# Token halves across the seam between two layers, with GpSimd adding residuals and squares

## The chip, the cores and the metric

The kernel runs on one core of one Trainium2 chip. Its time is the device time of one execution in microseconds (us). A core has five engines with queues of their own that meet only through semaphores: TensorE (PE in the rows; PEld is its weight load), VectorE (DVE), ScalarE (ACT), GpSimd (POOL) and SyncE (SP). Matmuls write to PSUM, the others read from it (POOL doesn't in this kernel). Before the change the median of three runs was 1852.86 us.

## The reference

Two transformer blocks over 512 tokens of width 2048, in float32. Around the change it computes the end of the first block and the start of the second:

```python
def _rms_norm(x, g):
    xf = x.astype(jnp.float32)
    y = xf * lax.rsqrt(jnp.mean(xf * xf, axis=-1, keepdims=True) + NORM_EPS)
    return (y * g.astype(jnp.float32)).astype(x.dtype)

def _hybrid_layer(...):          # first block
    ...
    o = jnp.concatenate([o_mla, o_fox], axis=-1) @ w_out
    return x + _rms_norm(o, g_post)

def second_block(x, ...):
    ...
        h = _rmsnorm(x, norm_g[l])
        proj = h @ w_in[l]
```

The first block's output projection `o @ w_out` needs all of its 2048 columns before the norm of a token is known; then the residual x is added, and the result is both the residual of the second block and, normed, the input of its projection.

## The kernel before, in words

Activations lie transposed: the feature on the partitions, 16 tiles (`KT`) of 128 features, each 512 tokens wide (`S`). A float32 product is made of three matmuls (`three`, L421 to L423): high part times high part, low part of the activation (`xl`) times high part of the weight, and high part (`xh`) times low part of the weight (`wl`). Weights come in units of 128 x 1024 through four slots of `raw`, `wh` and `wl`: SP loads `raw`, ACT rounds it to `wh` (L979, `act_hi`), DVE forms `wl` = raw - wh (L1433, `lo`), PE uses both and counts `w_used`, and then the slot may be refilled. Each engine works through a list written out by hand; the order in the code is the order on the engine, and semaphores count.

The first output projection makes 16 strips of 128 output features, each from 16 x 3 matmuls of 512 columns into one of two PSUM banks. DVE copies a strip out (L1902), ACT squares it (L1241), DVE adds the squares into `acc` (L1896). After strip 15 PE sums `acc` and the last squares over the partitions for each of four groups of 128 tokens (`pe_token_sums`, L552 and L556). DVE and ACT make the inverse root (`token_rms`, L1539 to L1547, with the square root at L1021) and put it on the diagonal of `gate` (L1550); PE spreads it over the partitions (`pe_spread`, L564) and runs six warm-up matmuls that nothing reads (L715).

Then every tile j goes through this chain: DVE scales it by g_post and the spread factor (L1924, `scale_tile`; the factor lies in PSUM); the residual is added, for tiles 0 and 1 by DVE from `xr1` (L1930), for tiles 2 to 15 by an accumulating DMA from DRAM that POOL's queue issues (L389); ACT makes `xh` (L1258) and the tile's squares (L1261); DVE makes `xl` (L1599, `x_rest`) and adds the squares (L1605, `square_in`). POOL also issues four stores of the new residual (L383). PE takes the tiles in order (`pe_four`): each is used at once for four outputs in four PSUM banks, 12 matmuls a tile. Two tiles use one weight unit, `U_CMPIN` + 0 to 7. Before unit 7 stands the sum over the squares (`pe_sum`, L546), which needs those of all 16 tiles; its result scales the projections that follow. At the very end of the kernel the same norm is already worked in two token halves, with strips of 256 columns (L960, L948, L952, L2248), and POOL scales some of the output tiles (L416).

Of the kernel before, what the change touches and what calls it, by code (L numbers as in the profile page):

```python
# [20 lines left out]
F32 = mybir.dt.float32  # L21
# [70 lines left out]
WARM_FIRST, WARM_MID = 5, 6  # L92
# [37 lines left out]
def _build(nc, d, ctx):  # L130
# [43 lines left out]
    sq = [place("sq0", [P, S], offset=at["prob"] + 2048), place("sq1", [P, S], offset=at["prob"] + 4096)]  # L174
# [43 lines left out]
    xr1 = place("xr1", [P, 2, S], offset=at["y"])  # L218

# [5 lines left out]
    kv0 = at["next"]  # L225

# [81 lines left out]
    scaled, part_done = sem("scaled"), sem("part_done")  # L308
    low_out, low_in = sem("low_out"), sem("low_in")
# [3 lines left out]
    four_done, raw_first, first_hi, first_lo = sem("four_done"), sem("raw_first"), sem("first_hi"), sem("first_lo")  # L313
    block = ctx.enter_context(nc.Block())
# [50 lines left out]
    def _(g):  # L365
# [9 lines left out]
        g.dma_start(xr1[:, :, :], d["xt"][:, 0:2, :]).then_inc(xr1_in, 16)  # L375
        g.dma_start(cos2[:, :], d["cos_a"]).then_inc(tab2_in, 16)
        g.dma_start(sin2[:, :], d["sin_a"]).then_inc(tab2_in, 16)

        def x_is_added(j):
            g.wait_ge(x_added[j % 4], 16 * (j // 4 + (j % 4 >= 2)))  # L380
# [167 lines left out]
    def pe_token_sums(pe, i, squared):  # L548

        pe.wait_ge(acc_ready, i + 1)  # L550
        for t in range(NQ):
            pe.matmul(px[:, t:t + 1], acc[:, P * t:P * t + P], ones[:, 0:1], start=t == 0, stop=False,  # L552
                      skip_group_check=True)
# [6 lines left out]
    def pe_spread(pe, k_, banks):  # L560

        for out in banks:
            pe.wait_ge(diag_done, NQ * (k_ + 1))
            pe.matmul(out[:, :], ones[:, :], gate[:, :], start=True, stop=True).then_inc(spread, 1)  # L564

    @block.tensor
    def _(pe):
# [141 lines left out]
        with pe.Fori(1, KT // 2 - 1) as i:  # L709
# [172 lines left out]
        def b_pair(p, u, n_, steps):  # L882
# [38 lines left out]
        for steps, strips in ((range(12, 15), (0,)), (range(12, 15), (1,)), (range(15, KT), (0, 1))):  # L921
            pe_together(pe, U_OUT2, N_OUT2, steps, 4 * KT - 6, strips=strips)
# [21 lines left out]
        def half_sums(hf):  # L944

            pe.wait_ge(acc_ready, 6 + hf)
            for t in (2 * hf, 2 * hf + 1):
                pe.matmul(px[:, t:t + 1], acc[:, P * t:P * t + P], ones[:, 0:1], start=t == 2 * hf, stop=False,  # L948
                          skip_group_check=True)
            pe.wait_ge(ev_act, N_OUT2 + KT - 4 + 2 * hf)  # L950
            for t in (2 * hf, 2 * hf + 1):
                ins = pe.matmul(px[:, t:t + 1], e_t[:, P * t:P * t + P], ones[:, 0:1], start=False,  # L952
                                stop=t == 2 * hf + 1, skip_group_check=True)
            ins.then_inc(sum_done, 1)
# [69 lines left out]
    def _(a):  # L1024
# [221 lines left out]
        with a.Fori(0, KT // 2 - 1) as i:  # L1246
            two_strips(At(U_OUT1 + 4, i, 4), lambda j: out_square(
                N_OUT1 + 2 + j + i * 2, o[:, bass.ds(2 * i + 2 + j, 1), :].rearrange("p a n -> p (a n)")))
        act_hi(a, At(U_CMPIN + 2))
        act_hi(a, At(U_CMPIN + 3))  # L1250
        act_root(a, 3)

        for j in range(KT):
            if j < 2:
                a.wait_ge(xn_done, j + 1)
            else:
                a.wait_ge(x_added[j % 4], 16 * (j // 4 + (j % 4 >= 2)))
# [162 lines left out]
        for hf in range(2):  # L1420
# [3 lines left out]
            act_root(a, 5 + hf, 2 * hf, 2 * hf + 2)  # L1424
            a.wait_ge(spread, 2 + 2 * hf)
# [128 lines left out]
    def _(v_):  # L1554
# [343 lines left out]
        def out1(first, i, last=False, banks=(pj[N_OUT1 % 2], pj[1 - N_OUT1 % 2])):  # L1898
            def evac(j, used):
# [16 lines left out]
        two_strips(At(U_CMPIN - 4), out1(14, 0, True))  # L1916
        token_rms(v_, 3)
        v_.memset(acc[:, :], 0.0)
        lo(v_, At(U_CMPIN + 2))
        lo(v_, At(U_CMPIN + 3))  # L1920
        v_.wait_ge(spread, 1)

        def scale_tile(j):
            ins = v_.scalar_tensor_tensor(o[:, j, :], o[:, j, :], c("g_post", j), po[:, :], ALU.mult, ALU.mult)  # L1924
            if j >= 2:
                ins.then_inc(scaled, 1)

        def residual(j):
            v_.drain()
            v_.tensor_tensor(o[:, j, :], o[:, j, :], xr1[:, j, :], ALU.add).then_inc(xn_done, 1)  # L1930

        scale_tile(0)
        v_.wait_ge(xr1_in, 16)
        residual(0)
        scale_tile(2)
        scale_tile(1)
        x_rest(0, o[:, 0, :], c("g_2", 0), 3 * KT - 6)
        residual(1)
        scale_tile(3)
        for j in range(KT):  # L1940
            if j + 4 < KT:
                scale_tile(j + 4)
            if j:
                x_rest(j, o[:, j, :], c("g_2", j), 3 * KT - 6)
            if j:
                square_in(j - 1, KT)
            if j in (5, 7, 9, 11):
                lo(v_, At(U_CMPIN + (j + 3) // 2))
        square_in(KT - 1, KT)
# [456 lines left out]
```

## Time and profile before

| what | value |
|---|---|
| median of three runs | 1852.86 us (1852.66 to 1852.92) |
| the profiled execution | 1853.12 us, span 1851.4 us |
| PE, DVE, ACT, POOL busy | 98%, 57%, 36%, 2% of the span |
| last matmul of the first projection starts | 955.20 us |
| sum matmul before unit 7 starts | 1007.88 us |

The span runs from the first to the last instruction of the profiled execution; the time is a little longer. Times in the rows are microseconds from the span's start. A busy PE is a matmul in flight: records of neighbouring matmuls overlap, so the distance from start to start tells the rate. An idle time in brackets is what the engine waited before the row, and for whom.

### The profile page before, as it was taken

To read this page: it belongs to the slowest core of one execution; us is meant where nothing else is said; L and a number is where in the kernel's file an instruction comes from. 1 tells how busy PE (TensorE), PEld (TensorE's weight loads), DVE (VectorE), ACT (ScalarE), POOL (GpSimd) and SP (SyncE) were. 2 spreads that over 40 slices of the span, in tenths; PEclk is the share of its full clock that TensorE was granted. 3 is DMA by queue.
4 is the path that set the end of the run, shared out by engine and by line. 5 is a ranking of instruction groups with operands and counts; after the bars stand their busy time and mean duration, and the time that the engine had idled before them with its cause. 6 is when DMAs were issued, how large, how long until landed. Compare 5 with 4: busy or idle time off the path is not lost.

```text
span 1851.4 us, 25537 instructions
## 1 busy us (share of the span) xinstructions
PE 1823.4 (98%) x9060; PEld 1514.8 (82%) x9060; DVE 1047.4 (57%) x1768; ACT 665.6 (36%) x1279; POOL 36.3 (2%) x58
## 2 busy tenths in 40 slices
PE   9999999999999999999999999999999999999997
PEld 7788888888888887878868887888888888888887
DVE  7643434444433787853348954766767566665334
ACT  6532332322223544432226342433433333443222
POOL 0000000000000000000002000000000000000001
PEclk9999999999999999999999999999999999999998
DMA  6322222222232333232237363211112222124333
GB/s 237 106 86 91 79 79 91 86 84 82 89 102 80 126 114 113 91 112 93 91 101 218 102 227 124 70 57 57 68 57 69 92 68 79 66 70 136 115 115 102
DMA packets 56021, 186.16 MB, mean 101 GB/s; under 512 B 6688, under 2 KB 11168, under 8 KB 55456
## 3 DMA queue, kind: packets, MB, share of 16 engines
q1 hardware_dynamic: 51328, 170.78, 27.6%
q0 software_dynamic: 4640, 14.68, 3.0%
q8 instruction: 33, 0.54, 0.1%
q14 instruction: 20, 0.16, 0.0%
HBM read 177.05 MB, written 8.39 MB: 100 GB/s over the span
## 4 chain that ended last, share of the span: by engine, by line
PE 90%; DVE 5%; DVEq 2%; ACT 1%; issue 1%; POOL 0%; POOLq 0%; ACTq 0%
PE strip L421 23%; PE strip L423 22%; PE strip L422 22%; PE scores L421 4%; PE scores L422 3%; PE scores L423 3%; PE outputs L423 2%; PE outputs L422 2%; PE outputs L421 1%; PE scores L476 1%; PE scores L869 1%; PE scores L828 1%; PE scores L897 1%; DVE wl L1433 1%; DVEq L1438 0%
## 5 line engine op out<-in xcount | busy, mean ns | idle before, releaser
L421 PE MATMUL strip<-xh,wh 128*128 128x512 f32 (+1 forms) x1976 | 779.7, 395 | 5.7 <-DVE xl L1825 3.2
L423 PE MATMUL strip<-xh,wl 128*128 128x512 f32 (+1 forms) x1976 | 768.0, 389 | 0.0
L422 PE MATMUL strip<-xl,wh 128*128 128x512 f32 (+1 forms) x1976 | 767.2, 388 | 0.0
L421 PEld LDWEIGHTS strip<-xh,wh 128*128 128x128 f32 x1976 | 371.9, 188 | 82.4 <-DVE xl L1825 4.8
L423 PEld LDWEIGHTS strip<-xh,wl 128*128 128x128 f32 x1976 | 371.6, 188 | 77.3
L422 PEld LDWEIGHTS strip<-xl,wh 128*128 128x128 f32 x1976 | 372.3, 188 | 72.7 <-issue 0.7
L1433 DVE TENSOR_TENSOR wl<-raw,wh 128x1024 fp32r<-128x1024 f32 (+3 forms) x306 | 354.7, 1177 | 119.1 <-ACT wh L979 118.2
L979 ACT ACTIVATE wh<-raw 128x1024 fp32r<-128x1024 f32 (+3 forms) x308 | 306.9, 1023 | 109.7 <-PE strip L423 107.1
L1001 ACT ACTIVATE prob<-scores,nms 128x128 f32<-128x128 f32 (+3 forms) x128 | 65.9, 532 | 129.7 <-DVE nms L1481 129.7
L1241 ACT ACTIVATE e_t<-o 128x512 f32 (+1 forms) x30 | 19.0, 632 | 222.0 <-DVE o L1902 118.1
L421 PE MATMUL scores<-xh,wh 128*128 128x512 f32 (+1 forms) x240 | 91.6, 382 | 0.0
L423 PE MATMUL scores<-xh,wl 128*128 128x512 f32 (+1 forms) x240 | 90.1, 375 | 0.0
L422 PE MATMUL scores<-xl,wh 128*128 128x512 f32 (+1 forms) x240 | 90.0, 375 | 0.0
L1441 DVE TENSOR_TENSOR y<-strip,rb 128x512 f32<-128x512 f32 x45 | 31.1, 692 | 75.7 <-PE strip L423 73.1
L1479 DVE TENSOR_REDUCE nm<-scores 128x1 f32<-128x128 f32 (+1 forms) x96 | 41.2, 485 | 55.1 <-PE scores L457 54.3
L984 ACT ACTIVATE q_h<-y 128x512 fp32r<-128x512 f32 x24 | 15.2, 632 | 145.8 <-DVE y L1454 107.2
L994 ACT ACTIVATE e_t<-y 128x512 f32<-128x512 f32 x32 | 20.5, 641 | 127.4 <-DVE y L1441 127.4
L1505 DVE TENSOR_TENSOR ptl<-scores,pth 128x512 fp32r<-128x512 f32 (+3 forms) x128 | 53.8, 483 | 9.7 <-ACT pth L1009 9.6
L421 PEld LDWEIGHTS scores<-xh,wh 128*128 128x128 f32 x240 | 45.2, 188 | 9.0 <-issue 0.5
L422 PEld LDWEIGHTS scores<-xl,wh 128*128 128x128 f32 x240 | 45.2, 188 | 8.7 <-issue 0.7
L423 PEld LDWEIGHTS scores<-xh,wl 128*128 128x128 f32 x240 | 45.2, 188 | 8.1
L1902 DVE COPY o<-strip 128x512 f32 (+1 forms) x14 | 9.7, 692 | 74.0 <-PE strip L423 73.9
(426 smaller groups left out, 1875.6 us busy)
## 6 DMA issues: line engine op xcount, KB each, us to landing
raw<-in_w SPq DMA_DIRECT2D x308, 512.0 KB, 3.2
xn<-o POOLq DMA_DIRECT2D x4, 1024.0 KB, 7.8
xr<-xn POOLq DMA_DIRECT2D x16, 256.0 KB, 3.0
o<-in_xt SPq DMA_DIRECT2D x7, 512.0 KB, 7.9
o<-in_xt POOLq DMA_DIRECT2D x14, 256.0 KB, 6.3
out<-o SPq DMA_DIRECT2D x14, 256.0 KB, 2.7
raw<-in_w SPq DMA_DIRECT2D x2, 256.0 KB, 4.6
o<-in_xt SPq DMA_DIRECT2D x2, 256.0 KB, 5.1
```

The costliest lines, as they stand in the source:

```text
L421: pe.matmul(out, ah, bh, start=first, stop=False, skip_group_check=shared)
L422: pe.matmul(out, ah, bl, start=False, stop=False, skip_group_check=shared)
L423: return pe.matmul(out, al, bh, start=False, stop=last, skip_group_check=shared)
L476: ins = pe.transpose(sb[t][:, P * (w - t):P * (w - t) + P], prob[:, ROW[w] + P * t:ROW[w] + P * t + P], ident[:, :])
L979: a.activation(wh[s][:, :cols], raw[s][:, :cols], ACT.Copy).then_inc(w_hi, 1)
L994: a.activation(e_t[:, :], src, ACT.Tanh, scale=0.5).then_inc(ev_act, 1)
L1001: a.activation(prob[:, ROW[t]:ROW[t] + w], sb[t][:, pre[t]:pre[t] + w], ACT.Exp, bias=nms[:, t:t + 1], scale=scale, accum_out=lsum[:, t:t ...
L1241: a.activation(e_t[:, :], src, ACT.Square).then_inc(ev_act, 1)
L1433: v_.tensor_tensor(wl[s][:, :cols], raw[s][:, :cols], wh[s][:, :cols].bitcast(F32), ALU.subtract)\
L1441: v_.tensor_tensor(dst, src[:, :], times[:, :], ALU.mult).then_inc(y_done, 1)
L1479: v_.tensor_reduce(nm[:, t:t + 1], sb[t][:, 0:P * (t + 1)], AX.X, ALU.max, negate=True)
L1505: v_.tensor_tensor(ptl[:, cols], sb[t][:, 0:w], pth[:, cols].bitcast(F32), ALU.subtract)\
```

## The change

- The last two strips (14 and 15) are made in token halves of 256 columns: both for tokens 0 to 255 first, then both for tokens 256 to 511. The token sums of the first half stand inside strip 14's second half, and its spread ahead of strip 15's second half.
- The first six tiles (`HT`) of the second layer's input are scaled, added, split and multiplied in halves too: all six for the first half of the tokens, then all six for the second. The second half's token sums come after tile 1's first half, its spread after tile 3's. The warm-up matmuls are gone.
- The residuals of the six tiles come from `xr1`, now six tiles wide, and POOL adds them (12 additions of 256 columns). Tiles 6 to 15 still get theirs by an accumulating DMA.
- The sum of squares goes from DVE to POOL, into its own `acc_mid`: 12 additions of 256 columns and ten of 512. The sum matmul waits for POOL's last one. The squares have four buffers instead of two.

```diff
-        for j in range(2, KT):
-            if j >= 6:
-                x_is_added(j - 4)
-            g.wait_ge(scaled, j - 1)
-            g.dma_start(o[:, j, :], d["xt"][:, j, :], accum_op=ALU.add).then_inc(x_added[j % 4], 16)
-            if j == 7:
-                g.wait_ge(xn_done, 2)
-            if j in (7, 11, 15):
-                xn_store(j - 7)
+        def residual(hf, j):
+            g.wait_ge(scaled, HT * hf + j + 1)
+            part = o[:, j, TOKENS[hf]]
+            g.tensor_tensor(part, part, xr1[:, j, TOKENS[hf]], ALU.add).then_inc(xn_done, 1)
+        def x_added_in(j):
+            if j - 4 >= HT:
+                x_is_added(j - 4)
+            g.wait_ge(scaled, HT + j + 1)
+            g.dma_start(o[:, j, :], d["xt"][:, j, :], accum_op=ALU.add).then_inc(x_added[j % 4], 16)
+        def square_half(hf, j):
+            g.drain()
+            g.wait_ge(sq_done, KT + HT * hf + j + 1)
+            g.tensor_tensor(acc_mid[:, TOKENS[hf]], acc_mid[:, TOKENS[hf]], sq_part(hf, j), ALU.add).then_inc(sq_used, 1)
+        def square(j):
+            g.drain()
+            g.wait_ge(sq_done, KT + HT + j + 1)
+            g.tensor_tensor(acc_mid[:, :], acc_mid[:, :], sq[j % 4][:, :], ALU.add).then_inc(sq_used, 1)
...
+        for j in range(HT, KT):
+            if j + 4 < KT:
+                x_added_in(j + 4)
+            if j == 8:
+                xn_store(4)
+            if j == 12:
+                xn_store(8)
+            square(j)
...
-        pe_token_sums(pe, 3, N_OUT1 + KT)
-        pe_spread(pe, 0, (po,))
-        for i in range(WARM_MID):
-            pe.matmul(px[:, :], ones[:, :], gate[:, :], start=True, stop=True)
-        pe_four(pe, U_CMPIN, 3 * KT - 6, sb, summed=(4, 7))
+        out1_half(0, 0, range(KT))
+        out1_half(0, 1, range(KT))
+        out1_half(1, 0, range(5))
+        pe_half_sums(pe, 0, 4, (half_sq, 2))
+        out1_half(1, 0, range(5, KT))
+        pe.wait_ge(diag_done, 2)
+        pe.matmul(po[:, 0:256], ones[:, :], gate[:, 0:256], start=True, stop=True).then_inc(spread, 1)
+        out1_half(1, 1, range(KT))
+        def aside(j):
+            if j == 1:
+                pe_half_sums(pe, 1, 5, (ev_act, N_OUT1 + KT))
+            if j == 3:
+                pe.wait_ge(diag_done, NQ)
+                pe.matmul(px[:, :], ones[:, :], gate[:, :], start=True, stop=True).then_inc(spread, 1)
+        pe_mid(pe, U_CMPIN, sb, aside)
...
+        for hf in range(2):
+            for j in range(HT):
+                pe.wait_ge(x_lo, X_MID + HT * hf + j + 1)
+                if hf == 0 and j % 2 == 0:
+                    pe.wait_ge(w_lo, u0 + j // 2 + 1)
+                for s in range(4):
+                    ins = tile(j, s, TOKENS[hf], hf == 0 and j == 0, False)
+                if hf == 1 and j % 2 == 1:
+                    ins.then_inc(w_used, 1)
+                if hf == 0:
+                    aside(j)
+        for u in range(HT // 2, 8):
+            if u == 7:
+                pe.wait_ge(sq_used, KT + HT + KT)
+                pe.matmul(px[:, :], ones[:, :], acc_mid[:, :], start=True, stop=True).then_inc(sum_done, 1)
...
+            scale_half(1, j)
+        rest_half(1, 0)
+        scale_half(1, 3)
+        rest_half(1, 1)
+        scale_half(1, 4)
+        rest_half(1, 2)
+        scale_half(1, 5)
+        scale_tile(6)
+        rest_half(1, 3)
+        scale_tile(7)
+        rest_half(1, 4)
+        rest_half(1, 5)
+        lo(v_, At(U_CMPIN + 4))
+        scale_tile(8)
+        scale_tile(9)
+        for j in range(HT, KT):
+            x_rest(j, o[:, j, :], c("g_2", j), X_MID + HT)
             if j + 4 < KT:
                 scale_tile(j + 4)
-            if j:
-                square_in(j - 1, KT)
```

ACT's list follows: half squares for the strips, then `xh_half` and `sq_half` for the six tiles, with the second half's square root behind `xh_half(0, 5)`.

POOL's queue at this place, before. `in_xt` is the first layer's input in DRAM, `xn` the new residual in DRAM:

```order
L389 DMA o<-in_xt 128x512 x6
L383 DMA xn<-o 128x2048
L389 DMA o<-in_xt 128x512 x4
L383 DMA xn<-o 128x2048
L389 DMA o<-in_xt 128x512 x4
L383 DMA xn<-o 128x2048 x2
```

The same place after, from the second half's third residual on (`xr_135` is `xr1`, `sq_87` and `sq_88` are two of the four buffers of squares):

```order
L392 TENSOR_TENSOR o<-o,xr_135 128x256
L401 DMA o<-in_xt 128x512
L392 TENSOR_TENSOR o<-o,xr_135 128x256
L401 DMA o<-in_xt 128x512
L392 TENSOR_TENSOR o<-o,xr_135 128x256
L406 TENSOR_TENSOR acc_mid<-acc_mid,sq_87 128x256
L392 TENSOR_TENSOR o<-o,xr_135 128x256
L401 DMA o<-in_xt 128x512
L406 TENSOR_TENSOR acc_mid<-acc_mid,sq_88 128x256
L401 DMA o<-in_xt 128x512
L406 TENSOR_TENSOR acc_mid<-acc_mid,sq_88 128x256
```

The DMA issues now stand in one queue with additions: residuals ahead of each issue, and sums of squares between them.

DVE's list before, once the factor is spread:

```order
L1924 SCALAR_TENSOR_TENSOR o<-o,cvec,outputs 128x512
L1930 TENSOR_TENSOR o<-o,xr_128 128x512
L1924 SCALAR_TENSOR_TENSOR o<-o,cvec,outputs 128x512 x2
L1599 SCALAR_TENSOR_TENSOR xl<-o,cvec,xh 128x512
L1930 TENSOR_TENSOR o<-o,xr_128 128x512
L1924 SCALAR_TENSOR_TENSOR o<-o,cvec,outputs 128x512 x3
L1599 SCALAR_TENSOR_TENSOR xl<-o,cvec,xh 128x512
L1605 TENSOR_TENSOR acc<-acc,sq_85 128x512
```

DVE's list after, once the second half's factor is spread (L2076 scales a half tile, L2085 a whole one, L2081 makes half of `xl`, L1584 is `lo`):

```order
L2076 SCALAR_TENSOR_TENSOR o<-o,cvec,odds 128x256 x3
L2081 SCALAR_TENSOR_TENSOR xl<-o,cvec,xh 128x256
L2076 SCALAR_TENSOR_TENSOR o<-o,cvec,odds 128x256
L2081 SCALAR_TENSOR_TENSOR xl<-o,cvec,xh 128x256
L2076 SCALAR_TENSOR_TENSOR o<-o,cvec,odds 128x256
L2081 SCALAR_TENSOR_TENSOR xl<-o,cvec,xh 128x256
L2076 SCALAR_TENSOR_TENSOR o<-o,cvec,odds 128x256
L2085 SCALAR_TENSOR_TENSOR o<-o,cvec,odds 128x512
L2081 SCALAR_TENSOR_TENSOR xl<-o,cvec,xh 128x256
L2085 SCALAR_TENSOR_TENSOR o<-o,cvec,odds 128x512
L2081 SCALAR_TENSOR_TENSOR xl<-o,cvec,xh 128x256 x2
L1584 TENSOR_TENSOR wl_59<-raw_51,wh_55 128x1024
```

The residual and the sum of squares are gone from DVE; tile 6's scaling stands behind three halves of `xl`, and tile 8's behind all six and a weight unit.

## Rows read from the trace of the kernel before

**Rows 1.** The page's first part: busy time, share and instructions of each engine.
```profile
PE 1823.4 (98%) x9060; PEld 1514.8 (82%) x9060; DVE 1047.4 (57%) x1768; ACT 665.6 (36%) x1279; POOL 36.3 (2%) x58
```
**Rows 2.** Windows: length, busy of PE, PEld, DVE, ACT, POOL, clock, DMA share, GB/s.
```profile
940.00:955.40 15.40, 15.40 (x69) 12.78 (x68) 3.75 (x4) 2.53 (x3) 0.00 (x0) 1.00 0.36 115
955.40:969.40 14.00, 10.42 (x32) 5.45 (x30) 10.63 (x22) 5.10 (x8) 1.46 (x2) 0.76 0.34 90
```
**Rows 3.** Window of DVE alone: length, DVE busy, clock, DMA share, GB/s.
```profile
969.30:1003.90 34.60, 32.81 (x46) 1.00 1.01 259
```
**Rows 4.** Timeline of PE at the gap and the sum: start, duration, instruction.
```profile
939.79 0.39 PE L421 MATMUL strip<-xh,wh 128*128 128x512 f32 x1
...
955.20 0.39 PE L423 MATMUL strip<-xh,wl 128*128 128x512 f32 x1
...
969.36 0.80 PE L421 MATMUL scores<-xh,wh 128*128 128x512 f32 x1
969.99 0.39 PE L422 MATMUL scores<-xl,wh 128*128 128x512 f32 x1
...
1007.88 1.02 PE L546 MATMUL odds<-acc,ones 128*128 128x512 f32 x2
...
1008.97 0.40 PE L422 MATMUL scores<-xl,wh 128*128 128x512 f32 x1
```
**Rows 5.** Timeline of PE near the end: half strips, half sums between, half spread.
```profile
1824.27 0.28 PE L421 MATMUL scores<-xh,wh 128*128 128x256 f32 x1
...
1827.03 0.28 PE L423 MATMUL scores<-xh,wl 128*128 128x256 f32 x1
...
1827.96 0.36 PE L421 MATMUL scores<-xh,wh 128*128 128x256 f32 x1
...
1830.91 0.60 PE L960 MATMUL outputs<-gate,ones 128*128 128x256 f32 x2
...
1831.47 0.28 PE L422 MATMUL scores<-xl,wh 128*128 128x256 f32 x1
```
**Rows 6.** Timeline of DVE and POOL near the end: operations of 256 columns, gate.
```profile
1821.42 0.43 DVE L2257 TENSOR_TENSOR acc<-acc,e_t 128x256 f32<-128x256 f32 x1 [2.22 <-ACT e_t L1423]
...
1828.57 0.17 DVE L1541 RECIPROCAL rinv<-nms 128x2 f32<-128x2 f32 x1 [0.27 <-ACT nms L1021]
...
1829.52 0.48 DVE L1550 TENSOR_SCALAR gate<-ident,rinv 128x128 f32<-128x128 f32 x2
...
1832.08 3.71 POOL L416 TENSOR_TENSOR o<-o,rb 128x256 f32<-128x256 f32 x5 [17.06 <-ACT rb L1426]
1832.27 0.83 DVE L2257 TENSOR_TENSOR acc<-acc,e_t 128x256 f32<-128x256 f32 x1 [0.73 <-ACT e_t L1423]
1833.23 4.40 DVE L2242 SCALAR_TENSOR_TENSOR o<-o,cvec,outputs 128x256 f32<-128x256 f32 x11
...
1843.60 3.45 POOL L416 TENSOR_TENSOR o<-o,rb 128x256 f32<-128x256 f32 x5 [7.82 <-ACT rb L1426]
```
**Rows 7.** Timeline in the second layer's input: one tile's xh, one weight remainder.
```profile
970.50 0.72 ACT L1258 ACTIVATE xh<-o,cvec 128x512 fp32r<-128x512 f32 x1 [1.34 <-DMA o<-in_xt]
...
980.00 1.22 DVE L1433 TENSOR_TENSOR wl<-raw,wh 128x1024 fp32r<-128x1024 f32 x1
```
**Rows 8.** Tile o on POOL: minimum, median, maximum of the operation (ns), of landing (us).
```profile
L416 POOL TENSOR_TENSOR o<-o,rb x10: 722/730/914, 1832.1 to 1846.3; 128x256 f32<-128x256 f32 x10
...
DMA to landing us min/median/max: 4.2/6.5/9.4
```
**Rows 9.** POOL's memsets (group and timeline) and two DMA issues in a row.
```profile
L366 POOL MEMSET nrt<- 128x512 f32 x1 | 0.5, 524 | 0.3 <-POOLq L2397 0.3
...
800.21 0.95 POOL L374 MEMSET blk<- 128x1024 f32 x1 [752.76 <-DVE o L1512]
...
974.61 0.87 POOL L389 DMA_DIRECT2D o<-in_xt  x1 [1.24 <-DVE o L1924]
975.15 0.89 POOL L383 DMA_DIRECT2D xn<-o  x1
```

More of the change, by code:

```diff
@@ L225, in _build @@
     kv0 = at["next"]
+    xr1 = place("xr1", [P, HT, S], offset=kv0)
     def group_kv(g, where):
@@ new lines, in _ @@
+        for j in range(HT):
+            residual(0, j)
+            if j >= 3:
+                square_half(0, j - 3)
+        residual(1, 0)
+        square_half(0, 3)
+        residual(1, 1)
+        square_half(0, 4)
+        residual(1, 2)
+        x_added_in(6)
+        residual(1, 3)
+        x_added_in(7)
+        residual(1, 4)
+        square_half(0, 5)
+        residual(1, 5)
+        x_added_in(8)
+        square_half(1, 0)
+        x_added_in(9)
+        for j in range(1, HT):
+            square_half(1, j)
@@ L546, in pe_sum, with pe_half_sums @@
         pe.matmul(px[:, :], ones[:, :], squares[:, :], start=True, stop=True).then_inc(sum_done, 1)
[L548 to L552, printed above, removed]
+    def pe_half_sums(pe, hf, added, squared):
+        pe.wait_ge(acc_ready, added)
+        for t in (2 * hf, 2 * hf + 1):
+            pe.matmul(px[:, t:t + 1], acc[:, P * t:P * t + P], ones[:, 0:1], start=t == 2 * hf, stop=False,
@@ L553, in pe_token_sums, with pe_half_strip @@
                       skip_group_check=True)
-        pe.wait_ge(ev_act, squared)
-        for t in range(NQ):
-            ins = pe.matmul(px[:, t:t + 1], e_t[:, P * t:P * t + P], ones[:, 0:1], start=False, stop=t == NQ - 1,
+        pe.wait_ge(*squared)
+        for t in (2 * hf, 2 * hf + 1):
+            ins = pe.matmul(px[:, t:t + 1], e_t[:, P * t:P * t + P], ones[:, 0:1], start=False, stop=t == 2 * hf + 1,
                             skip_group_check=True)
         ins.then_inc(sum_done, 1)
[L560 to L564, printed above, removed]
+    def pe_half_strip(pe, u0, out, hf, steps):
+        for k_ in steps:
+            u = u0 + k_ // 8
+            if k_ % 8 == 0:
+                pe.wait_ge(w_lo, u + 1)
+            cols = slice(P * (k_ % 8), P * (k_ % 8) + P)
+            ins = three(pe, out[:, 0:256], wh[u % SLOTS][:, cols], wl[u % SLOTS][:, cols], xh[:, k_, TOKENS[hf]],
+                        xl[:, k_, TOKENS[hf]], k_ == 0, k_ == KT - 1)
+            if hf == 1 and k_ % 8 == 7:
+                ins.then_inc(w_used, 1)
+        if hf == 0 and k_ == KT - 1:
+            ins.then_inc(part_done, 1)
@@ L944, in half_sums @@
         def half_sums(hf):
[L946 to L954, printed above, removed]
+            pe_half_sums(pe, hf, 6 + hf, (ev_act, N_OUT2 + KT - 4 + 2 * hf))
         def half_spread(hf, banks):
@@ L1896, in add_square, with out1 @@
             v_.tensor_tensor(acc[:, :], acc[:, :], e_t[:, :], ALU.add).then_inc(r_done, 1)
-        def out1(first, i, last=False, banks=(pj[N_OUT1 % 2], pj[1 - N_OUT1 % 2])):
+        def out1(first, i, banks=(pj[N_OUT1 % 2], pj[1 - N_OUT1 % 2])):
             def evac(j, used):
@@ L1915, in _ @@
             two_strips(At(U_OUT1 + 4, i, 4), out1(2, i))
-        two_strips(At(U_CMPIN - 4), out1(14, 0, True))
-        token_rms(v_, 3)
-        v_.memset(acc[:, :], 0.0)
+        for j in range(2):
+            lo(v_, At(U_CMPIN - 2 + j))
+        out1_half(0, 0)
+        half_add(0)
+        out1_half(0, 1)
+        token_rms(v_, 3, 0, 2)
+        out1_half(1, 0)
+        v_.wait_ge(spread, 1)
+        scale_half(0, 0)
+        scale_half(0, 1)
+        half_add(1)
+        v_.drain().then_inc(r_done, 1)
@@ L1923, in scale_tile @@
[L1923 to L1937, printed above, removed]
@@ L1938, in _ @@
-        residual(1)
-        scale_tile(3)
-        for j in range(KT):
+        v_.wait_ge(spread, 2)
+        for j in range(3):
+            scale_half(1, j)
[13 more added lines that the diff above has]
+        scale_tile(9)
```

199 lines of the change are left out of this document (152 added, 47 removed).

## The prediction

> **What bounds the kernel now.** I read the page first. TensorE (PE) is busy 98% of the span and VectorE (DVE) 57%, ScalarE 36%, GpSimd (POOL) 2% [rows 1]. So a change pays only where PE does no useful matmuls, or costs where it makes PE wait. The table by stage shows the place [rows 2]: before 955.4 us PE is full at a granted clock of 1.00; from 955.4 to 969.4 it is busy 10.42 of 14.00 us at 0.76; then it is full again. Then the timeline of PE [rows 4]: the last strip matmul starts at 955.20; token sums, the wait for the root, the spread and six warm-up matmuls fill the gap; the first matmul of the second layer is recorded at 969.36, the one behind it at 969.99. At one matmul per 0.2266 us (below) the last strip matmul ends its turn at 955.43 and the first new one really ran at 969.76. The useful work stops for 14.33 us. From there to the sum matmul at 1007.88 PE waits for nothing, while DVE is nearly full (32.81 of 34.60 us) [rows 3] and POOL only issues DMAs.
>
> **PE's own ledger.** 512-column matmuls come every (955.20 - 939.79)/68 = 0.2266 us [rows 4]; 256-column ones every (1827.03 - 1824.27)/23 = 0.120 us [rows 5]. Two strips (96) and six tiles of four outputs (72) are split: 168 x (2 x 0.120 - 0.2266) = +2.25 us. Two half token sums now lie between matmuls: 1827.96 - (1827.03 + 0.12) = 0.81 each, 1.62 [rows 5]. The 256-column spread costs (1831.47 - 1830.91) - 0.12 = 0.44 [rows 5]. The 512-column one costs what the sum matmul does, 1008.97 - 0.23 - 1007.88 = 0.86 [rows 4]. Together 5.17 us, against 14.33 removed (the warm-ups lie in these). If PE never waited, the sum would start 9.16 us earlier, at 998.7, and the kernel would take 1843.7. All that follows asks whether the others can feed it.
>
> **The first halves.** The strips begin at 955.43 - 96 x 0.2266 = 933.68. The first half's spread comes after 144 half matmuls and the sums: 951.8 to 952.2. Scaling takes 0.40 a half tile (4.40/11) [rows 6], so POOL gets its first residual at 952.9. POOL's 256-column op comes every 3.45/5 = 0.69 us [rows 6]. Until residual 5 it has eight ops (six residuals, two adds): 5.5 us.
>
> Now the port. The group of five POOL ops during which a DVE add with two SBUF inputs ran took 3.71 us, the other 3.45; that DVE add took 0.83 us, and 0.43 when POOL was still; the eleven DVE ops whose factor lay in PSUM kept 0.40 [rows 6]. So two-input DVE ops and POOL's take turns, and POOL lost 0.26, the add's 256 elements at about 1 ns. I scale it by elements: 0.27 for 256, 0.53 for 512, 1.07 for 1024. The Trainium skill (SBUF — State Buffer, Who interferes with whom) states this as an exclusive lock, in which the later of the two blocks fully; the trace agrees, and the rule speaks against this change, since it puts tensor work on POOL beside a DVE that makes weight and activation remainders from two SBUF inputs. Without turns the sum would be the first rival's.
>
> POOL loses three weight remainders (3.2) and six small ones (1.6), and waits 0.7 for scaling: residual 5 ends at 952.9 + 5.5 + 3.2 + 1.6 + 0.7 = 963.9. Behind it on ScalarE's queue stand xh (0.72 for a whole tile [rows 7]; a half is put at six tenths of it, 0.43) and then the square root of the second half's sums, put at 0.2 for two columns; DVE's small ops and two gates take (1829.52 + 0.48) - 1828.57 = 1.43 [rows 6]: gate ready at 966.1. PE, which ends its last half strip at 933.68 + 23.04 + 0.81 + 0.44 = 957.97, wants it after four half tiles and the sums, at 964.5. It waits 1.6 us. The spread ends at 967.0, DVE does one rest and one weight remainder before scaling, and POOL starts the second halves at 968.2.
>
> **POOL's ledger from 968.2 to the sum,** which now waits for POOL's last add:
> - six residuals x 0.69 = 4.1
> - nine half adds x 0.73 (each waits for the one before to end, 0.722 in the trace [rows 8]) = 6.6
> - ten whole-tile adds: no 512-column POOL op with two inputs is in the trace. Between 0.72 (size costs nothing) and 1.44 (twice the record). The two memsets, 0.524 for 512 columns and 0.95 for 1024 [rows 9], leave a fixed 0.1; (0.69 - 0.1) x 2 + 0.1 = 1.28, I take 1.30: 13.0
> - ten accumulating DMAs and three stores: between 0.54 (975.15 - 974.61, two starts in a row) and 0.87 (a record's length) [rows 9]; nearer to neither, I take 0.70: 9.1
> - three times POOL stands still because the tile whose DMA is next is scaled only behind rests that wait for POOL's own residual: xh 0.43, rest 0.43, scale 0.40, tile scale 0.74, with handoffs 2.3; the next without the half scale 1.9; the third with a weight remainder of 1.22 [rows 7], 3.0: 7.2
> - DVE's two-input ops in this stretch: 6 x 0.27 + 4 x 1.07 + 10 x 0.53 = 11.2. Some fall while POOL issues or idles, and some wait for POOL instead. Between 0 and 11.2; I take two fifths, 4.5.
> Sum 44.5: the sum matmul starts at 1012.7 instead of 1007.88, +4.8 us. Unit 7's 24 matmuls behind it and all that follows hang on it as before.
>
> The Trainium skill (GPSIMD Engine Reference, Elementwise — side-by-side cycle accounting) gives about 2.6 cycles an element and 4497 ns for 2048; an estimate from it for 512 is near 1.2 us. No row here shows one, and with it the sum would be about 1 us less.
>
> DVE loses 16 adds of 0.69 and two residuals; this is worth nothing, since it now waits for POOL. Four accumulating DMAs of 256 KB fewer relieve a stage whose DMA share is 1.01 [rows 3]; their landing, 4.2 to 9.4 us [rows 8], stays under the four-tile lead, so I count nothing. The longer xr1 load is issued behind the memset of 800.21 us [rows 9], 150 us ahead: nothing; its cover would have to shrink by all of that.
>
> The profiled execution took 1853.12 for a span of 1851.4; the median of the three runs is 1852.86. The difference applies to all alike: 1852.86 + 4.8 = 1857.7.
>
> **Rivals.**
> 1. *The turns at the port cost little.* For it: most POOL time in the trace is undisturbed. Against: the 0.83. Then 4.5 goes, and of the first halves' 4.8 the 1.6 that PE waited: 1857.7 - 6.1 = 1851.6.
> 2. *PE stays the bound* (the other side). Mechanism: DMA issues run under the adds (0.54 and overlapped), a whole add is near 0.9, and POOL's still times are covered. POOL must save 1012.7 - 998.7 = 14.0: issues 7, adds 4, port 3. It decides once POOL's last add ends before 998.7. Time 1844; half of that saving still gives about 1850.7.
> 3. *POOL at its upper bounds:* issues at 0.87 (+2.2), adds 1.44 (+1.4), port seven tenths (+3.3): 1864.6; with half of it 1861.
> 4. *The clock.* Over the gap of before, where PE stood and then ran warm-ups, the granted clock was 0.76, between its two levels [rows 2]. PE would now wait in bits of 2 us with work between, so I expect 1.00; if it lost as much as in the gap, 0.24 of 14 us, 3.4 go unless POOL is late anyway: 1861 at most.
>
> **Chances.** This kernel can be told from no change by about 0.2%, 3.7 us: faster is below 1849.2, slower above 1856.6. Forecast 0.55 (own range 1854 to 1861; 0.12 of it below 1856.6), rival 1 0.19 (same but 0.02), rival 2 0.16, rivals 3 and 4 0.10. Slower 0.43 + 0.10 = 0.53; faster 0.18; same 0.29. The range leaves out the upper part of rival 3 and the lower of rival 2: 1847.5 to 1862.
>
> **What would show it.** Right: POOL nearly full from 968 to 1012; the sum matmul idle before it, with POOL's whole-tile add as releaser; half tiles of the second half waiting on xl; DVE's two-input ops longer than 0.75 and 1.22 beside POOL's; whole POOL adds near 1.3. Wrong: no idle time of PE after 957 (rival 2), POOL ops at 0.69 with DVE ops at their old lengths (rival 1), a granted clock under 1.00 between 966 and 990 (rival 4), or PE waiting for the DMAs of tiles 6 to 15, which I have at nothing.

## The result, and the profile after

The changed kernel took 1898.94 us (median of four runs, 1898.39 to 1899.32), the kernel before on the same chip 1852.89 (1852.66 to 1853.4): ratio 1.0248, 95% interval 1.023 to 1.0266. The forecast was 1857.7. The sign was right, and the loss is 46 us where 4.8 were forecast. The profiled execution took 1898.84 us with a span of 1897.1.

The profile of the changed kernel is called after. Its page, busy time, share and instructions of each engine, beside [rows 1]:

```profile
PE 1827.5 (96%) x9218; PEld 1524.0 (80%) x9218; DVE 1044.5 (55%) x1769; ACT 669.1 (35%) x1294; POOL 66.5 (4%) x89
```

PE's busy time is nearly what it was; 46 us were added in which it stands. The table of waits of PE from 930 to 1100 us (line, releaser, total us, times, longest):

```profile
PE scores L474 <- DVE xl L1750: 19.4, 5, 6.3
PE odds L649 <- POOL acc_mid L411: 15.8, 1, 15.8
PE scores L474 <- DVE xl L2081: 6.6, 3, 2.4
PE odds L833 <- DVE gate L1701: 1.4, 1, 1.4
```

The same table for POOL:

```profile
POOL o L392 <- DVE o L2076: 154.5, 4, 149.9
POOL acc_mid L411 <- issue: 31.0, 10, 6.9
POOL acc_mid L406 <- issue: 12.1, 12, 4.0
POOL o L401 <- DVE o L2085: 7.6, 3, 3.2
```

Here lies the answer. The three waits for `L2085` (the scaling of a whole tile) are the 7.6 us that the forecast had as 7.2. But 43.1 us stand ahead of the 22 square adds with "issue" as their releaser, which means that no semaphore in the profile ended them. The instruction in front of each add is `g.drain()`. The timeline of POOL shows what it waited for (start, duration, instruction, idle before it):

```profile
968.36 0.74 POOL L392 TENSOR_TENSOR o<-o,xr 128x256 f32<-128x256 f32 x1 [3.24 <-DVE o L2076]
969.25 0.74 POOL L406 TENSOR_TENSOR acc_mid<-acc_mid,sq 128x256 f32<-128x256 f32 x1 [0.16 <-issue]
...
987.50 0.87 POOL L401 DMA_DIRECT2D o<-in_xt  x1 [3.16 <-DVE o L2085]
992.41 0.73 POOL L406 TENSOR_TENSOR acc_mid<-acc_mid,sq 128x256 f32<-128x256 f32 x1 [4.05 <-issue]
993.10 0.86 POOL L401 DMA_DIRECT2D o<-in_xt  x1
997.49 0.71 POOL L406 TENSOR_TENSOR acc_mid<-acc_mid,sq 128x256 f32<-128x256 f32 x1 [3.53 <-issue]
998.37 0.72 POOL L406 TENSOR_TENSOR acc_mid<-acc_mid,sq 128x256 f32<-128x256 f32 x1 [0.17 <-issue]
...
1001.95 0.60 POOL L414 DMA_DIRECT2D xn<-o  x1
1002.54 0.89 POOL L401 DMA_DIRECT2D o<-in_xt  x1
1010.33 1.26 POOL L411 TENSOR_TENSOR acc_mid<-acc_mid,sq 128x512 f32<-128x512 f32 x1 [6.90 <-issue]
...
1031.19 0.86 POOL L401 DMA_DIRECT2D o<-in_xt  x1
1035.48 1.27 POOL L411 TENSOR_TENSOR acc_mid<-acc_mid,sq 128x512 f32<-128x512 f32 x1 [3.44 <-issue]
1036.71 0.85 POOL L401 DMA_DIRECT2D o<-in_xt  x1
```

Behind additions only, the idle time ahead of an add is 0.16 us. Right behind an accumulating DMA it is 3.4 to 4.1 us, behind a 1 MB store and such a DMA 6.9, behind such a DMA and a store 5.65 (the add of 1024.25). A DMA lands when its data have arrived and its semaphore has counted them. ScalarE waits for just that before it makes `xh` of a tile, so its rows tell the time of the landing:

```profile
1035.33 0.72 ACT L1410 ACTIVATE xh<-o,cvec 128x512 fp32r<-128x512 f32 x1 [3.43 <-DMA o<-in_xt]
```

The tile issued at 1031.19 has landed by 1035.33, and POOL's add starts at 1035.48. The same holds for the other whole adds that have a tile's DMA right in front of them: each starts 0.15 to 0.19 us behind ScalarE's start on that tile. So the drain ends with the landing. A queue in which issue and landing overlapped has become a chain: issue, landing, add, next issue. Its period is 1036.71 - 1031.19 = 5.5 us a tile, 8.3 to 9.0 where a store lies in it; PE needs 12 x 0.2266 = 2.7 us a tile.

PE at the spread and at the sum, timeline (answers to [rows 4]):

```profile
966.41 1.13 PE L833 MATMUL odds<-gate,ones 128*128 128x512 f32 x2 [1.40 <-DVE gate L1701]
...
1052.24 2.08 PE L649 MATMUL odds<-acc_mid,ones 128*128 128x512 f32 x2 [15.78 <-POOL acc_mid L411]
```

And the windows of after in the columns of [rows 2]:

```profile
955.40:970.00 14.60, 13.20 (x106) 12.52 (x105) 13.20 (x25) 8.11 (x18) 9.06 (x10) 1.00 0.39 126
970.00:990.00 20.00, 11.87 (x82) 10.33 (x81) 9.90 (x17) 7.72 (x15) 8.07 (x10) 1.00 0.33 68
990.00:1010.00 20.00, 11.93 (x43) 8.99 (x42) 6.10 (x8) 3.95 (x6) 6.84 (x9) 0.83 0.58 143
1010.00:1052.00 42.00, 16.38 (x48) 11.76 (x48) 10.62 (x10) 11.29 (x15) 17.61 (x17) 0.68 0.42 106
```

The gap itself is filled: 13.20 of 14.60 us at a clock of 1.00, where it was 10.42 of 14.00 at 0.76. What was won there is lost from 970 on. No engine is full there: POOL, which the table of waits names, is busy 17.6 of 42 us. When neither PE nor its releaser is busy, the time goes into a wait that the busy times don't hold.

### The profile page after: what moved, and what is told of

Same layout as the page of the kernel before. It is cut to its first block, busy times and chain, and to the rows that moved or that the text cites. A ratio compares the mean times of both kernels' runs of the same rounds, so it can differ in the third digit from the quotient of the medians.

```text
span 1897.1 us, 25891 instructions
## 1 busy us (share of the span) xinstructions
PE 1827.5 (96%) x9218; PEld 1524.0 (80%) x9218; DVE 1044.5 (55%) x1769; ACT 669.1 (35%) x1294; POOL 66.5 (4%) x89
## 4 chain that ended last, share of the span: by engine, by line
PE 83%; DVE 6%; issue 4%; DVEq 2%; ACT 2%; POOL 1%; POOLq 1%; DMA 0%; SPq 0%; ACTq 0%
PE strip L474 22%; PE strip L476 22%; PE strip L475 22%; PE scores L474 2%; PE scores L475 2%; PE scores L476 2%; PE outputs L476 2%; PE outputs L475 2%; PE outputs L474 1%; PE scores L529 1%; DVE wl L1584 1%; PE scores L988 1%; PE scores L947 1%; PE scores L1016 1%; POOLq L404 1%
## 5 line engine op out<-in xcount | busy, mean ns | idle before, releaser
L474 PEld LDWEIGHTS strip<-xh,wh 128*128 128x128 f32 x2008 | 377.9, 188 | 81.5 <-DVE xl L1976 4.8
L476 PEld LDWEIGHTS strip<-xh,wl 128*128 128x128 f32 x2008 | 377.5, 188 | 76.3
L475 PEld LDWEIGHTS strip<-xl,wh 128*128 128x128 f32 x2008 | 378.1, 188 | 71.6 <-issue 0.7
L1584 DVE TENSOR_TENSOR wl<-raw,wh 128x1024 fp32r<-128x1024 f32 (+3 forms) x306 | 355.8, 1180 | 120.9 <-ACT wh L1090 120.0
L474 PE MATMUL scores<-xh,wh 128*128 128x512 f32 (+1 forms) x264 | 100.5, 381 | 26.6 <-DVE xl L1750 19.7
L475 PE MATMUL scores<-xl,wh 128*128 128x512 f32 (+1 forms) x264 | 96.8, 367 | 0.0
L476 PE MATMUL scores<-xh,wl 128*128 128x512 f32 (+1 forms) x264 | 96.6, 366 | 0.0
L474 PEld LDWEIGHTS scores<-xh,wh 128*128 128x128 f32 x264 | 51.6, 196 | 39.6 <-DVE xl L1750 23.3
L475 PEld LDWEIGHTS scores<-xl,wh 128*128 128x128 f32 x264 | 51.7, 196 | 8.2 <-issue 0.8
L476 PEld LDWEIGHTS scores<-xh,wl 128*128 128x128 f32 x264 | 51.4, 195 | 8.0
L1120 ACT ACTIVATE pth<-scores 128x512 fp32r<-128x512 f32 (+3 forms) x128 | 45.1, 437 | 12.3 <-PE scores L947 9.7
```

The source lines that it names most:

```text
L474: pe.matmul(out, ah, bh, start=first, stop=False, skip_group_check=shared)
L475: pe.matmul(out, ah, bl, start=False, stop=False, skip_group_check=shared)
L476: return pe.matmul(out, al, bh, start=False, stop=last, skip_group_check=shared)
L1120: a.activation(pth[:, COL[t]:COL[t] + w], sb[t][:, 0:w], ACT.Copy).then_inc(pt_hi, 1)
L1584: v_.tensor_tensor(wl[s][:, :cols], raw[s][:, :cols], wh[s][:, :cols].bitcast(F32), ALU.subtract)\
```

## The experiments

**1. Another wait in place of the drain.** Theory A: the drain waits for POOL's own DMAs. Theory B: POOL's work itself (adds, issues, the port) is dearer than forecast. All 22 drains become a wait on the semaphore that the add before has raised:

```diff
         def square_half(hf, j):
-            g.drain()
+            g.wait_ge(sq_used, KT + HT * hf + j)
...
         def square(j):
-            g.drain()
+            g.wait_ge(sq_used, KT + HT + j)
```

> The changed kernel with POOL's 22 drains ahead of its adds replaced by a wait on the semaphore that the add before it counts (sq_used); nothing else. Theory A (the drain holds POOL until its own accumulating DMAs have landed, 4.2 to 4.9 us each): the 41 us beyond my forecast go, POOL's ledger holds, about 1857.7 (1854 to 1862), and POOL's idle times of 3.4 to 7.8 us ahead of its adds shrink below 1 us save for the three waits for scaling. Theory B (POOL's adds are late for another reason: the landing of tiles' DMAs and ScalarE's waits for the square buffers): stays above 1890.

Measured 1864.89 us (1863.74 to 1865.43), ratio 1.0063 [1.0046, 1.0079]. 34.1 of the 46 us are gone with nothing else changed, and theory B's 1890 is far off; but the time stands 2.9 us above theory A's range, so something else was mis-sized too. POOL now issues while the adds run:

```profile
992.80 0.60 POOL L414 DMA_DIRECT2D xn<-o  x1
993.39 0.89 POOL L401 DMA_DIRECT2D o<-in_xt  x1
993.97 1.63 POOL L411 TENSOR_TENSOR acc_mid<-acc_mid,sq 128x512 f32<-128x512 f32 x1
995.21 1.23 POOL L401 DMA_DIRECT2D o<-in_xt  x1
```

The waits of PE from 930 to 1100 us:

```profile
PE scores L474 <- DVE xl L1750: 6.2, 2, 4.3
PE scores L474 <- DVE xl L2081: 3.8, 2, 2.4
PE odds L649 <- POOL acc_mid L411: 2.0, 1, 2.0
PE odds L833 <- DVE gate L1701: 1.3, 1, 1.3
```

**2. The drain alone, in the kernel before.** One drain behind each accumulating DMA, nothing else of the change:

```diff
             g.dma_start(o[:, j, :], d["xt"][:, j, :], accum_op=ALU.add).then_inc(x_added[j % 4], 16)
+            g.drain()
```

> The kernel before, with one drain on POOL behind each of the 14 accumulating DMA issues; no other change. Theory A: each issue follows the landing of the one before, one tile per about 4.4 + 0.5 = 4.9 us, the last lands near 966 + 14 x 4.9 = 1034.6 instead of about 1001; PE starts the sum near 1036 to 1038 instead of 1007.9: 1880 to 1884. Theory B: a drain costs 0.16 us as behind an add and is hidden: 1853.

Measured 1891.91 us (1889.67 to 1893.15), ratio 1.0212 [1.0195, 1.0229]: 39 us slower, 8 above the top of what was expected, with no additions on POOL in this stage. Its timeline:

```profile
981.99 0.86 POOL L389 DMA_DIRECT2D o<-in_xt  x1 [3.67 <-issue]
...
996.79 0.56 POOL L383 DMA_DIRECT2D xn<-o  x1 [4.12 <-issue]
997.34 0.90 POOL L389 DMA_DIRECT2D o<-in_xt  x1
1004.75 0.86 POOL L389 DMA_DIRECT2D o<-in_xt  x1 [6.51 <-issue]
```

Much the same 3.7 to 4.4 us ahead of the next issue, and 6.5 with a store in front. So the cost is the drain's, and needs neither an add nor a busy port. The expectation was too low because it left out the stores: with one in front of a DMA the step to the next issue is 7.4 us (1004.75 - 997.34) instead of 4.9, and that happens twice; the first issue was also 1.4 us later than assumed. The sum matmul starts at 1043.88.

**3. Only the half adds keep their drains.** Experiment 1's edit in `square` alone, so twelve of 22 stay:

```diff
         def square(j):
-            g.drain()
+            g.wait_ge(sq_used, KT + HT + j)
```

> The changed kernel with the drains ahead of the ten whole-tile adds replaced by the wait on the add before; the 12 drains ahead of half adds stay, three of which stand behind a DMA issue. Theory A: in the trace of the changed kernel those three waited 2.52, 4.05 and 3.53 us (10 together) and the whole-tile ones 31 us in all; so most of the loss goes and some 5 to 10 us stay against the kernel without any: 1863 to 1868. Theory B: no change from 1899.

Measured 1871.25 us (1870.47 to 1874.97), ratio 1.0105 [1.0088, 1.0122]. The ten drains of the whole-tile adds cost 27.7 us, the twelve others 6.4: 34.1 together. Of the twelve, three stand behind an issue (of tiles 7, 8 and 9); in after these three waited 2.52, 4.05 and 3.53 us. The time is 3.3 us above the expected range. The 6.4 us lie within the 5 to 10 expected; the kernel without any drain, to which they are added, came out slower than assumed.

**4. The stores out of the way.** Experiment 1 still stood 7.2 us above the forecast. Its longest wait of PE:

```profile
1003.98 0.50 PE L474 MATMUL scores<-xh,wh 128*128 128x512 f32 x1 [4.29 <-DVE xl L1750]
```

This is behind tile 10, whose DMA was issued at 993.39 right behind the 1 MB store of 992.80. On ScalarE, `xh` of that tile began when it had landed:

```profile
1002.42 0.72 ACT L1410 ACTIVATE xh<-o,cvec 128x512 fp32r<-128x512 f32 x1 [8.89 <-DMA o<-in_xt]
```

That is 9.0 us from issue to landing, against 4.2 us for the median of these DMAs in after. Experiment 4 takes experiment 1 and moves the four stores of `xn` behind the last accumulating DMA:

```diff
         g.wait_ge(xn_done, 2 * HT)
-        xn_store(0)
...
-            if j == 8:
-                xn_store(4)
-            if j == 12:
-                xn_store(8)
...
-        xn_store(12)
+        for k0 in range(0, KT, 4):
+            xn_store(k0)
```

> The kernel without POOL's drains (e1_sem_for_drain), with the four 1 MB stores of the new residual moved behind the last accumulating DMA instead of between them. Theory A (in e1 the store issued 0.6 us ahead of tile 10's accumulating DMA makes that land 9.0 us after its issue, and PE waits 4.3 us for tile 10): landing near 5 us, PE's wait goes: about 1861 (1864.9 less 4). Theory B (the landing is slow since the DMA engines are full of weights): 1865 as before.

Measured 1861.61 us (1860.88 to 1862.05), ratio 1.0044 [1.0027, 1.0061]: 3.3 us less, as expected. Tile 10's DMA, issued at 993.55, had landed when its `xh` began at 997.72, and PE's longest wait is 2.6 us, at a half tile. The weights are loaded as before and only the store has moved, so theory B falls. Whether the place in the queue or the store's mere traffic slowed the landing isn't told apart: from 993.5 to 1002.4 us the DMA share is 0.82, in experiment 1 it was 0.94.

**5. POOL without the sums.** Experiment 1 with all 22 adds in DVE's list (the stores as in the change). The line taken out is POOL's, the new ones are DVE's:

```diff
-            square(j)
...
+            if j < 9:
+                square_half(1, 2 * (j - 6))
+                square_half(1, 2 * (j - 6) + 1)
```

> e1_sem_for_drain with all 22 additions of squares moved from POOL to DVE's list (same tiles, same accumulator, stores where they are); POOL keeps 12 residuals, the DMAs and stores. Theory A (POOL's additions and their turns at the port cost PE time): the 2.0 us wait ahead of the sum and part of the waits for tiles go, 1858 to 1861. Theory B (the chain of scaling, residual, xh, xl and the landing alone holds PE): 1864 to 1866, PE's waits at the same tiles.

Measured 1859.87 us (1859.32 to 1861.01), ratio 1.0037 [1.0023, 1.0051]. 5.0 us less than experiment 1, within theory A's range. But the wait ahead of the sum did not go: PE now waits 2.8 us there for DVE's last add, so DVE is late in turn. What went is the long wait at tile 10, with the stores where they were: PE's longest wait at a whole tile is 1.4 us. POOL, free of adds, issues tile 10 at 986.91 instead of 993.39. So the adds and the store share that wait, and the gains of experiments 4 and 5 can't be added.

**6. DVE scales one or two places sooner,** on top of experiment 4, and POOL issues tiles 6 and 7 one residual later, so that no issue stands in front of a residual that DVE's next rest needs:

```diff
-        rest_half(1, 0)
         scale_half(1, 3)
-        rest_half(1, 1)
+        rest_half(1, 0)
         scale_half(1, 4)
-        rest_half(1, 2)
         scale_half(1, 5)
+        rest_half(1, 1)
         scale_tile(6)
```

> e4_stores_last with another order: DVE scales the half tiles 3 to 5 and the whole tiles 6 to 9 one or two places earlier, ahead of the rests that wait for POOL, and POOL does residual 3 ahead of tile 6's DMA issue. Theory A (my term of 7.2 us: POOL stands still for scalings that stand behind its own residuals): PE's waits at the fourth, fifth and seventh tile of the second half, 5.7 us in e1, mostly go: 5 us under e4, about 1856. Theory B (a wait that only moves): within 1.5 us of e4.

Measured 1856.55 us (1855.2 to 1858.18, ten runs), ratio 1.0016 [1.0006, 1.0026]: 5.1 us less than experiment 4. POOL stood still ahead of its DMA issues for 9.4 us in four places in experiment 4 and for 3.0 us in two here, and PE's waits for halves of `xl` fell from 5.0 to 2.1 us. The forecast had seen these waits, at 7.2 us. The edit moves items of both lists, so DVE's share and POOL's are not told apart.

**7. The ten whole-tile adds on DVE,** on top of experiment 6; POOL keeps residuals and half adds.

```diff
-            square(j)
...
+            for t in {9: (6,), 10: (7, 8), 11: (9,), 12: (10,), 13: (11,), 14: (12, 13), 15: (14,)}.get(j, ()):
+                square_tile(t)
+        square_tile(15)
```

> e6_scale_ahead with the ten whole-tile additions of squares moved from POOL to DVE; the 12 half additions stay on POOL. Theory A (what is left over the kernel before is POOL's queue: in e6 PE waits 1.9 us for POOL ahead of the sum, and 0.6 and 1.3 for tiles 10 and 11, whose xl and DMA issue stand behind POOL's whole adds): 1856.6 less 2 to 4, so 1853 to 1854.5. Theory B (DVE takes the same time with them): 1856 to 1858, the sum waiting for DVE.

Measured 1852.79 us (1849.46 to 1854.09) against 1854.13 for the kernel before in this comparison, ratio 0.9992 [0.9983, 1.0001]: equal. That is 3.8 us under experiment 6, where 2 to 4 were expected. PE's waits are down to 4.7 us in four places:

```profile
PE scores L469 <- DVE xl L2076: 2.1, 1, 2.1
PE odds L828 <- DVE gate L1696: 1.3, 1, 1.3
PE scores L469 <- DVE xl L1745: 0.7, 1, 0.7
PE odds L644 <- DVE acc_mid L2084: 0.6, 1, 0.6
```

**8. The second half's spread sooner,** on top of 7. The root stands one place earlier on ScalarE, POOL's first adds stand behind all six residuals, and one weight remainder behind the second halves. Theory A: the gate comes early enough and its wait goes. Theory B: it doesn't matter.

```diff
             residual(0, j)
-            if j >= 3:
-                square_half(0, j - 3)
+        for j in range(3):
+            square_half(0, j)
```

> e7_whole_adds_on_dve with the second half's norm sooner: its root on DVE and ScalarE ahead of the last two half tiles of the first half, POOL's first three half adds behind all six residuals, and the weight remainder of unit 3 behind the second half's scalings. Theory A (PE's 1.3 us wait for the second gate and the 2.1 us wait for the fourth half tile come from this order): 2 to 3 us under e7, about 1851. Theory B (these waits only move to the tiles behind them): within 1 us of e7.

Measured 1852.48 us (1850.87 to 1855.53), ratio 0.9994 [0.9985, 1.0003]: B. The wait at the gate stayed 1.4 us. Its chain on DVE began 0.5 us sooner (964.76 for 965.24), but two of its small operations on two columns now fell under POOL's three adds:

```profile
965.67 0.60 DVE L1691 SCALAR_TENSOR_TENSOR rinv<-rinv,nm 128x2 f32<-128x2 f32 x1
966.35 0.72 DVE L1693 SCALAR_TENSOR_TENSOR rinv<-rinv 128x2 f32<-128x2 f32 x1
```

In experiment 7, with POOL still, each took 0.16:

```profile
966.20 0.16 DVE L1691 SCALAR_TENSOR_TENSOR rinv<-rinv,nm 128x2 f32<-128x2 f32 x1
966.44 0.16 DVE L1693 SCALAR_TENSOR_TENSOR rinv<-rinv 128x2 f32<-128x2 f32 x1
```

The two end at 966.27 and 967.07, just when POOL's second and third add end (966.26 and 967.06). So each waited for the whole add in front of it.

**9. The half adds on DVE too,** on top of 8: only the residuals stay on POOL. In DVE's list:

```diff
-        scale_half(1, 5)
+        square_half(0, 0)
         rest_half(1, 1)
-        lo(v_, At(U_CMPIN + 3))
-        scale_tile(6)
+        scale_half(1, 5)
+        square_half(0, 1)
         rest_half(1, 2)
+        scale_tile(6)
```

> e8_second_spread_sooner with the 12 half additions of squares on DVE too, between its scalings and rests; POOL keeps the 12 residuals, ten accumulating DMAs and the stores. Theory A (POOL's adds hold up DVE's two-input operations at the shared port: in e8 two operations of two columns took 0.60 and 0.72 us instead of 0.16, and halves of xl up to 1.5 instead of 0.48): the second gate comes 1 us sooner and 1 to 2.5 us are gained, 1850 to 1851.5. Theory B (DVE's own 5 us more of work take back what the port gives): 1852 to 1854.

Measured 1853.89 us (1852.42 to 1855.73), ratio 1.0006 [0.9997, 1.0015] against 1852.9 for the kernel before in this comparison: theory B's range; theory A's gain did not come. The gate's wait fell to 0.4 us, but PE waits 4.8 us in four places for `xl` of whole tiles, the longest 3.0: the adds stand in DVE's list ahead of them.

**10. No residual halves.** Experiment 9, with the residual of tiles 0 to 5 left out of the computation, so that `xh` follows the scaling with no hop over POOL:

```diff
         def xh_half(hf, j):
-            a.wait_ge(xn_done, HT * hf + j + 1)
+            a.wait_ge(scaled, HT * hf + j + 1)
```

> e9_all_adds_on_dve without the 12 half residual additions for tiles 0 to 5 (ScalarE waits for the scaling instead; acc_mid is zeroed on DVE): the residual of six tiles is left out of the computation. It prices the hop over POOL. Theory A (scaling, then POOL, then ScalarE, then DVE again for every half tile is what keeps PE waiting; PE's own ledger allows 1843.7): PE's waits in tiles 0 to 5 go, 1846 to 1849. Theory B (DVE is the bound there): within 1.5 us of e9.

Measured 1850.85 us (1849.62 to 1851.95), ratio 0.9989 [0.998, 0.9998]. 3.0 us under experiment 9 (1.8 between the two profiled executions), between the two theories. So the hop costs some 2 to 3 us, with the turns at the port that POOL's 12 additions bring. Even without it PE's own ledger (1843.7) isn't reached: PE waits 4.8 us for `xl` of whole tiles, as in experiment 9, 1.1 us for one half and 0.7 us at the sum, 6.6 of the 7.2 us that are left.

## Why the prediction was right in sign and wrong in size

**The step that failed** is the second line of POOL's ledger: "nine half adds x 0.73 (each waits for the one before to end, 0.722 in the trace [rows 8])", and with it the ten whole adds. The text looked at the drain and took it for the end of the addition before it, 0.04 us (0.73 for an add, 0.69 for a residual). In after the drains from 968 on cost 43.1 less the 1.0 of the first halves, 42.1 us. The stretch from 968.36 to the end of the last add (1050.93 + 1.26 = 1052.19) took 83.8 us where the ledger has 44.5: 39.3 too much, which the drains' 42.1 more than cover. 39.5 us on the sum matmul (1052.24 for 1012.7) put 1857.7 at 1897.2. Of the 1.7 that remain, practically all (1.8) lie between the sum and the next strip (8.16 us, before 6.34), where PE started again at a granted clock of 0.81 in the window from 1052 to 1062. Experiments 1 to 3 show the cause: taken out it gives 34.1 us back, put in alone it costs 39.

**The sentence that closed the door** is "their landing, 4.2 to 9.4 us [rows 8], stays under the four-tile lead, so I count nothing". The landing was sized rightly; the lead was not there. The add of tile j stands behind the issue of tile j + 4, and a drain between them waits for that one. The upper bound of the rival with POOL's dearest prices (1864.6) had no term for it. Each drain should have had two prices: 0.04 us, and the landing of the DMA in front of it, 4.2 at the least by [rows 8]. Ten drains have a fresh issue in front of them (three of half adds, behind tiles 7, 8 and 9; six of whole adds, behind tiles 10 to 15; one more behind a store). 10 x 4.2 = 42 us would have been the price of these. They took 40.6, and the nine others 1.5 (0.16 or 0.17 each). That the two sums are so close is in part luck: one of the ten took 2.52 and two took 6.90 and 5.65, where a store was issued just ahead of the DMA or just behind it.

**The same sentence also failed in a second way.** A 256 KB DMA behind a 1 MB store of the same queue landed after 9.0 us and stopped PE for 4.3 us. [Rows 8] had the 9.4; with the drains gone this cost 3.3 us (experiment 4). The forecast counted nothing for it.

**The other steps, by the trace of after.** Last first-strip half and start of the second layer's tiles: 958.20, forecast 957.97. Wait at the second spread: 1.40, forecast 1.6. First residual of the second halves: 968.36, forecast 968.2. POOL's waits for scalings: 2.43, 2.03 and 3.16, forecast 2.3, 1.9 and 3.0. A whole add: 1.26, taken as 1.30. So the first halves and the unit prices held.

The port's turns were seen where the forecast put them, one row of each kind:

```profile
961.86 1.77 DVE L1584 TENSOR_TENSOR wl<-raw,wh 128x1024 fp32r<-128x1024 f32 x1
...
962.51 1.72 POOL L392 TENSOR_TENSOR o<-o,xr 128x256 f32<-128x256 f32 x1
```

1.77 for the 1.22 of [rows 7], and 1.72 for 0.74. This is the exclusive lock of the Trainium skill (SBUF — State Buffer, Who interferes with whom), and the trace of after agrees; how much of POOL's ledger it took is not settled, since the adds' move to DVE (experiments 5, 7 and 9) removes turns and POOL time at once.

**How much of the forecast is left once the drain is gone.** Experiment 1 is the change without it: 1864.9, 7.2 above the forecast and at the top of the third rival, though for other reasons than its dearest prices. The sum matmul starts at 1018.76, 6.1 late, and the drains had hidden this. 3.3 us are the store's landing. POOL stood still for 11.9 us in five places ahead of its issues, where the ledger has 7.2 in three; two of the five (2.56 and 1.76, for tiles 14 and 15) lie behind PE's long wait for tile 10, so these sizes overlap. What the clock took of it no run separates. The clock's rival came true in part: in the stretches that hold waits of 1.3 to 4.3 us PE was granted less. Windows of experiment 1 (length, PE busy, clock, DMA share, GB/s):

```profile
975.00:985.00 10.00, 6.22 (x38) 0.83 0.39 57
985.00:995.00 10.00, 8.11 (x29) 0.83 0.78 200
995.00:1008.00 13.00, 8.71 (x32) 0.87 1.00 255
```

The forecast expected 1.00 there. In after it was 1.00 from 970 to 990 us, with waits of 2.40, 1.99 and 2.24 us among them, and lower only from 997.5 on.

**Where the last of the 9.16 us went.** In experiment 7 the sum starts at 1007.89, where it did before, although PE's own ledger allows 998.7. Of these 9.2 us, 4.7 are the waits above. One more lies in front, in a start of the half strips at 934.76 instead of 933.86 (0.9). Behind the 2.1 us wait, which ends at 978.16, the clock fell, as the windows of experiment 7 show in the same columns:

```profile
978.50:981.00 2.50, 2.50 (x15) 0.54 0.48 65
981.00:984.00 3.00, 3.00 (x23) 0.81 0.91 136
```

By an estimate that is 0.46 x 2.5 + 0.19 x 3 = 1.7 us; from 984 the clock is 1.00 again. 1.9 remain open. The wait doesn't explain the fall by itself: experiment 6 has the same wait at the same half tile (2.14 us, to 977.20) and kept its clock, as its window shows in the columns of [rows 2]:

```profile
978.00:988.00 10.00, 8.78 (x53) 7.44 (x52) 10.00 (x12) 6.71 (x11) 9.58 (x9) 1.00 0.72 158
```

The 46 us by medians: drains 34.1; the store in front of tile 10's DMA 3.3 (experiment 4); scalings that waited behind rests 5.1 (experiment 6); whole-tile adds on POOL 3.8 (experiment 7). They sum to 46.3, and what is left is as fast as before. The order of removal matters for the shares, and the medians of the kernel before in these comparisons lie between 1852.7 and 1854.1, so each of the three small shares is good to about 1 us. The drain's stands by itself, since it was shown from both sides.

## What to carry to other kernels

Before an engine that issues DMAs is given arithmetic, read every instruction between the issues for what it waits on, a drain above all, and give it two prices: with nothing in flight, and with the DMA before it in flight. Order additions on such an engine by a semaphore that the addition itself raises, and keep large stores behind small transfers that someone is about to wait for. And when idle time has "issue" as its releaser while every engine is half empty, look at the instruction in front of it that the profile doesn't list.

## What the runs showed of the hardware that was not expected

- A drain on GpSimd took 0.16 us behind additions, 3.4 to 4.4 us right behind a 256 KB accumulating DMA of the same engine, 6.5 to 6.9 us where a 1 MB store was issued just ahead of that DMA, 5.7 us where one was issued just behind it, and 3.8 us behind a store alone (in after and experiment 2). It waits for the landing, not for the issue: in after the add starts 0.15 to 0.19 us behind ScalarE's start on the landed tile.
- A 256 KB accumulating DMA issued 0.59 us behind a 1 MB store in the same queue landed after 9.0 us (experiment 1), and after 4.2 us with the store moved away (experiment 4).
- The turns at the port don't scale down with size alone: DVE operations of two columns took 0.60 and 0.72 us beside POOL's additions (experiment 8), 0.16 without (experiment 7), and each ended when an addition did.
- After a wait of 2.1 us PE's granted clock was 0.54 in the next 2.5 us (experiment 7), near the lower of its two levels (1.2 of 2.4 GHz). After the same wait in experiment 6 it was 1.00, and after one of 2.40 us in after as well. So no run here tells from the length of such a wait whether the clock falls.
